# An even layer reordered: top-score selection unrolled, step sizes early, decay matrices on ScalarE in two buffers, query jobs a tile ahead

## The reference, cut to what matters

```python
def ssd_chunked(xh, dt, a, bm, cm):                  # chunks of 128 tokens, 8 heads, 2 groups
    x = (xh * dt[..., None])
    acum = jnp.cumsum(dt * a, axis=2)                # inside a chunk
    seg = acum[:, :, :, None] - acum[:, :, None]
    decay = jnp.exp(jnp.where(causal, seg, -jnp.inf))
    cb = jnp.einsum('bctgn,bcsgn->bctsg', cm, bm)
    y_diag = jnp.einsum('bctsgh,bcsghp->bctghp', cb[..., None] * decay, x)
    to_end = jnp.exp(acum[:, :, -1:] - acum)
    chunk_states = jnp.einsum('bclgn,bclghp->bcghpn', bm, x * to_end[..., None])
    ...                                              # scan: state * exp(acum[-1]) + chunk state
def dsa_attention(q, k, v, iq, ik, iw, rel_bias):
    score = sum over 4 index heads of relu(iq . ik) * iw         # 512 x 512, causal
    _, sel = lax.top_k(score, 128)                   # 128 keys for each query
    ...                                              # softmax attention over the selected keys
```

## Time and profile before

| | us |
|---|---|
| median of 3 runs | 1755.28 |
| lowest, highest | 1754.5, 1756.51 |
| the profiled execution, device time | 1753.81 |
| its span, first to last instruction | 1752.1 |
| TensorE busy | 1600.9 |
| VectorE busy | 448.1 |
| ScalarE busy | 388.9 |
| GpSimd busy | 199.5 |

### The profile page before, as it was taken

One profiled execution on the slowest core, in us unless ns is written; L12 is line 12 of the kernel. 1 busy time (PEld: TensorE's weight loads), 2 busy tenths in 40 slices (PEclk: granted clock), 3 DMA queues, 4 the chain that ended last, 5 costly groups with the idle time before them and its releaser, 6 DMA issues.

```text
span 1752.1 us, 20849 instructions
## 1 busy us (share of the span) xinstructions
PE 1600.9 (91%) x7890; PEld 757.1 (43%) x7890; DVE 448.1 (26%) x1152; ACT 388.9 (22%) x857; POOL 199.5 (11%) x286
## 2 busy tenths in 40 slices
PE   6995989979999999998399989999799999999993
PEld 3543665533333333333245447774433333333331
DVE  1475752430000000000403235552600000000002
ACT  2343252311111111111100125641211111111110
POOL 2240230000000000000101013320000000000000
PEclk9997989989999999999599999999899999999997
DMA  7120026259999999999813320024499999999995
GB/s 240 50 94 6 27 86 248 101 229 414 422 421 421 422 422 422 422 423 405 268 11 110 119 64 1 1 82 207 155 397 422 421 422 421 422 422 421 423 421 204
DMA packets 110919, 468.24 MB, mean 267 GB/s; under 512 B 34105, under 2 KB 40505, under 8 KB 61708
## 3 DMA queue, kind: packets, MB, share of 16 engines
q1 hardware_dynamic: 103564, 450.67, 64.3%
q10 hardware_dynamic: 2176, 8.39, 1.3%
q0 software_dynamic: 5120, 8.41, 1.3%
HBM read 456.91 MB, written 18.91 MB: 272 GB/s over the span
## 4 chain that ended last, share of the span: by engine, by line
PE 74%; DMA 10%; DVE 8%; issue 2%; SPq 2%; ACT 2%; POOL 1%; DVEq 0%; ACTq 0%; POOLq 0%
PE bank L1685 22%; PE bank L1698 10%; PE bank L1665 9%; PE bank L1333 8%; DMA arena<-in_moe_w_up 8%; PE bank L533 6%; PE bank L427 4%; PE bank L395 3%; PE bank L773 2%; PE bank L1675 2%; DVE arena L1113 2%; SPq L1637 2%; DVE m L1112 2%; PE bank L412 1%; PE bank L1691 1%
## 5 line engine op out<-in xcount | busy, mean ns | idle before, releaser
L1685 PE MATMUL bank<-arena 128*64 128x512 f32 x2048 | 452.7, 595 | 16.4 <-DMA arena<-in_moe_w_up 15.0
L1685 PEld LDWEIGHTS bank<-arena 128*64 128x64 f32 x2048 | 148.0, 137 | 311.7 <-issue 302.5
L1698 PE MATMUL bank<-arena 128*64 128x512 f32 x1024 | 230.6, 593 | 2.1 <-DVE arena L1787 2.1
L1783 DVE TENSOR_TENSOR arena<-arena,bank 128x256 f32<-128x256 f32 x64 | 27.0, 421 | 655.6 <-ACT arena L1773 655.6
L1704 POOL DMA_INDIRECT y_d<-arena,slot_row x64 | 62.6, 978 | 927.6 <-ACT arena L1778 914.0
L1665 PE MATMUL bank<-arena 128*64 128x512 bf16 x1152 | 153.7, 395 | 8.2 <-DVE arena L1658 8.2
L1333 PE MATMUL bank<-arena 128*128 128x512 f32 x320 | 140.7, 602 | 0.8 <-issue 0.8
L1698 PEld LDWEIGHTS bank<-arena 128*64 128x64 f32 x1024 | 71.6, 137 | 124.3 <-issue 110.8
L1773 ACT ACTIVATE arena<-bank 128x256 f32<-128x256 f32 x64 | 24.5, 383 | 420.1 <-PE bank L1685 420.1
L533 PE MATMUL bank<-arena 128*128 128x512 f32 x256 | 111.4, 593 | 0.0
L773 PE MATMUL bank<-arena 128*128 128x512 f32 (+1 forms) x288 | 106.8, 532 | 0.0
(11 more groups left out here) (279 smaller groups left out, 1450.6 us busy)
## 6 DMA issues: line engine op xcount, KB each, us to landing
arena<-in_moe_w_gate SPq DMA_DIRECT2D x64, 2048.0 KB, 21.0
arena<-in_moe_w_up SPq DMA_DIRECT2D x64, 2048.0 KB, 25.5
arena<-in_moe_w_down SPq DMA_DIRECT2D x64, 2048.0 KB, 24.2
arena<-in_even_w_in SPq DMA_DIRECT2D x4, 2048.0 KB, 8.5
arena<-y_d ACTq DMA_DIRECT2D x8, 1024.0 KB, 8.6
arena<-bias_row_d SPq DMA_DIRECT2D x2, 3584.0 KB, 11.9
arena<-in_odd_w_in SPq DMA_DIRECT2D x3, 2048.0 KB, 7.9
arena<-in_even_w_out SPq DMA_DIRECT2D x2, 2048.0 KB, 7.9
```

The costliest lines, as they stand in the source:

```text
L1685: mm = nc.tensor.matmul(bank[1][fh * CAP:(fh + 1) * CAP, :], xeT[:, j, half * CAP:(half + 1) * CAP], wgu[u][:, :, n, fh * FH:(fh + 1) * FH ...
L1698: mm = nc.tensor.matmul(bank[3][dh * CAP:(dh + 1) * CAP, :], hidT[:, j, fh * CAP:(fh + 1) * CAP], wd[u][:, n, dh * 512:(dh + 1) * 512], st ...
```

## The change

1. `take(i)` is written out: 16 pairs of `max` and `match_replace` in a straight line for each tile, no loop.
2. The three instructions of `raw_dt` stand ahead of the index scores. ScalarE's `softplus` stands after the taps of the fifth channel job. VectorE finishes `dt` and `dA` after tile 1 of the selection, and copies `acum`, `alast` and their difference after tile 2, for all tiles at once. TensorE makes the cumulated sums and the totals (with the matrix of ones) and the first tile's decay columns between the channel jobs and the z jobs. ScalarE takes the exponentials of all tiles at once, after the z jobs.
3. The x and B rows of the four tiles are turned into six different banks or halves (`x_bank`, `b_bank`), and evacuated in six copies where there were eight.
4. `seg` has two buffers. ScalarE makes it from the bank, as Relu(acum - column) and then Exp with scale -1 (8 Relus and 2 Exps for a tile); the 8 VectorE instructions, the copy of the last column and the subtraction go.
5. TensorE runs the query job of tile i+1 ahead of the state, decay and diagonal work of tile i; query head sums, scaling, turning and evacuating happen inside the loop, one or two tiles behind. `ssm_row(i-1)` moves behind seg times product of tile i, so that VectorE doesn't wait for the power at the end of a tile.
6. The four turns of Mamba rows move from before the attention's first unit to after its third to sixth group (`2 + i`), each with a wait for the last `ssm_row`. TensorE doesn't wait for `ssm_row` before the attention.
7. SyncE doesn't wait for the turned keys before it loads the second half of the output weight.

```diff
                 else:
                     self.finished(pe, u["needs"])
+                    if u["ready"]:
+                        pe.wait_ge(*u["ready"])
                     for k in range(4):
                         mm = nc.tensor.transpose(b[:, k * P:(k + 1) * P], u["src"][:, k * P:(k + 1) * P], ident[:])
...
-        seg = at(O_SS, SG, 4, P)
+        seg = [at(O_SS, SG, 4, P), at(O_SCORE + (NT - 1) * SEQ, SG, 4, P)]
         cbm = at(O_SS + 1024, SG, P)
...
         y2 = at(O_SS + 2304, DI)
         ssm_gain = at(O_SS + 2816, DI)
-        krn = at(O_SS + 3328, NT, P)
...
+
+            def queries(i):
+
+                b = q_bank(i)
+                if i in (0, 1):
+                    pe.wait_ge(S("tok_out"), (2, 4)[i])
+                else:
+                    pe.wait_ge(*((S("tok_out"), 5) if i == 2 else (S("sq"), 3)))
+                for k in range(KD):
+                    mm = nc.tensor.matmul(b[:, :], hT[:, k, i * P:(i + 1) * P], ew[0][:, k, :],
...
+            pe.wait_ge(S("dA"), 1)
+            pe.wait_ge(S("ix_relu"), len(SC))
+            for n, t_ in enumerate((tri, ones)):
+                mm = nc.tensor.matmul(bank[4][:, n * NT * SH:(n + 1) * NT * SH], t_[:], dA[:].rearrange("p i h -> p (i h)"),
+                                      start=True, stop=True)
+            mm.then_inc(S("acum_mm"), 1)
+            decays(0)
+            pe.wait_ge(S("ep_w3"), 16)
+            for i in range(NT):
+                tokens(J_Z + i, ew[1], (i,), DI)
+
+            pe.wait_ge(S("ep_ev"), J_Q)
+            pe.wait_ge(S("silu"), CT)
...
+            for i in range(NT):
...
+                    mm = nc.tensor.transpose(x_bank[i][:, j * P:(j + 1) * P], xbcS[:, j, i * P:(i + 1) * P], ident[:])
+                mm.then_inc(S("tok_turned"), 1)
+            for pair in range(2):
+                if pair:
+                    products(0)
...
+                for i in range(2):
...
+                mm.then_inc(S("tok_turned"), 1)
+            pe.wait_ge(S("ep_w4"), 16)
+            queries(0)
+            for i in range(NT):
+                if i < NT - 1:
+                    queries(i + 1)
                 if i >= 1:
                     pe.wait_ge(S("state"), i)
+                    pe.wait_ge(S("sq"), 2)
...
                 if i < NT - 1:
                     pe.wait_ge(S("xw"), i + 1)
+                    pe.wait_ge(S("tok_out"), 6)
...
                     mm.then_inc(S("st_mm"), 1)
+                    decays(i + 1)
+                    products(i + 1)
                 for g in range(SG):
...
+                if i == NT - 1:
+                    pe.wait_ge(S("kn"), 2)
...
+                    mm.then_inc(S("qk_turned"), 1)
                 if i >= 1:
...
+                    turn_queries(pe, i - 1)
+            turn_queries(pe, NT - 1)
             pe.wait_ge(S("qk_out"), NT + 1)
...
-            pe.wait_ge(S("ssm_row"), NT)
             even_att.pe(pe)
             outproj_pe(pe, even_att, "eo", mixT, e_wo, 0)
...
+            return i + 1 if i < 2 else i + 2
+
+        def q_bank(i):
+            return (bank[1], bank[4], bank[5], bank[4])[i]
+
+        def turn_queries(pe, i):
...
+                if c == CT // 2:
+                    softplus(act)
...
-                if i == 1:
-                    softplus()
...
+            act.wait_ge(S("acum"), 1)
+            nc.scalar.activation(eac[:], acum[:], ACT.Exp).then_inc(S("eac"), 1)
+            nc.scalar.activation(cdecay[:], alast[:], ACT.Exp).then_inc(S("eac"), 1)
+            nc.scalar.activation(to_end[:], to_end[:], ACT.Exp).then_inc(S("eac"), 1)
+            for i in range(NT):
+                act.wait_ge(S("tok_turned"), i + 1)
+                nc.scalar.activation(xtok[:, i, :], x_bank[i][:, :], ACT.Copy).then_inc(S("tok_out"), 1)
...
+            def decays(i):
+
+                if i >= 2:
+                    act.wait_ge(S("yd_mm"), i - 1)
                 for g in range(SG):
+                    act.wait_ge(S("abc_mm"), 2 * i + g + 1)
+                    for h in range(4):
...
+                        ins_ = nc.scalar.activation(seg[i % 2][:, g, h, :], bank[6 + g][:, h * P:(h + 1) * P], ACT.Relu,
+                                                    bias=acum[:, i, hh:hh + 1], scale=-1.0)
+                    ins_.then_inc(S("seg"), 1)
                     act.wait_ge(S("seg"), 2 * i + g + 1)
-                    nc.scalar.activation(seg[:, g], seg[:, g], ACT.Exp).then_inc(S("decay"), 1)
+                    nc.scalar.activation(seg[i % 2][:, g], seg[i % 2][:, g], ACT.Exp, scale=-1.0).then_inc(S("decay"), 1)
+
+            def queries(i):
                 act.wait_ge(S("ep_mm"), J_Q + i + 1)
-                nc.scalar.activation(qrows[:, i, :], bank[4 + i % 2][:, :], ACT.Copy).then_inc(S("ep_ev"), 1)
-                nc.scalar.activation(junk[:, i, :], bank[4 + i % 2][:, :], ACT.Square).then_inc(S("sq"), 1)
+                nc.scalar.activation(qrows[:, i, :], q_bank(i)[:, :], ACT.Copy).then_inc(S("ep_ev"), 1)
...
+            decays(0)
+            queries(0)
+            act.wait_ge(S("hgain"), 1)
+            for i in range(NT):
+                if i < NT - 1:
+                    queries(i + 1)
+                    decays(i + 1)
+                if i >= 2:
+                    turned_queries(i - 2)
                 act.wait_ge(S("y_gated"), i + 1)
                 for g in range(SG):
...
-            for i in range(NT):
+            head_norm(0, ssq[:, :, HEADS:])
+            for i in range(NT):
+                head_norm(i + 1, ssq[:, i:i + 1, 0:HEADS])
                 pool.wait_ge(S("y_sq"), 2 * i + 2)
...
+            dve.wait_ge(S("par_in"), 16 * 12)
...
+            v_.tensor_tensor(dt_e[:], dt_e[:], dt[:], ALU.max).then_inc(S("dt_abs"), 1)
...
-            def take(sc, n):
-                with dve.Fori(0, n // 16) as r:
-                    link.enter(r, 4)
-                    for _ in range(2):
-                        link(v_.max(m8[:], sc))
-                        link(v_.match_replace(sc, m8[:], sc, TAKEN))
-                    link.leave(n // 16)
...
+            def take(i):
+
...
+                for _ in range(TOPK // 8):
+                    link(v_.max(m8[:], sc))
+                    link(v_.match_replace(sc, m8[:], sc, TAKEN))
                 v_.tensor_scalar(selm[:, i, 0:L], sc, TAKEN / 2, NEG, ALU.is_gt, ALU.mult).then_inc(S("selm"), 1)
...
+            take(1)
...
                                     ALU.mult, ALU.mult).then_inc(S("dA"), 1)
+            take(2)
             dve.wait_ge(S("acum_mm"), 1)
-            v_.tensor_copy(acum[:], split(bank[3][:, 0:NT * SH], NT, SH)).then_inc(S("acum"), 1)
-            dve.wait_ge(S("acum"), 1)
+            sums = split(bank[4][:, 0:2 * NT * SH], 2, NT, SH)
+            link(v_.tensor_copy(acum[:], sums[:, 0]))
+            link(v_.tensor_copy(alast[:], sums[:, 1]))
+            v_.tensor_tensor(to_end[:], alast[:], acum[:], ALU.subtract).then_inc(S("acum"), 1)
+            take(3)
+
+            def key_sums():
...
-                for g in range(SG):
-                    dve.wait_ge(S("abc_mm"), 2 * i + g + 1)
-                    link(v_.tensor_copy(alast[:, 4 * g:4 * g + 4], split(bank[6 + g][:, :], 4, P)[:, :, P - 1]))
-                v_.tensor_tensor(to_end[:], alast[:], acum[:, i, :], ALU.subtract).then_inc(S("alast"), 1)
-                if i >= 1:
-                    dve.wait_ge(S("yd_mm"), i)
-                for g in range(SG):
-                    for h in range(4):
-                        hh = 4 * g + h
-                        ins_ = v_.tensor_scalar(seg[:, g, h, :], bank[6 + g][:, h * P:(h + 1) * P],
-                                                acum[:, i, hh:hh + 1], 0.0, ALU.subtract, ALU.min)
-                    ins_.then_inc(S("seg"), 1)
...
                 if i < NT - 1:
...
+                    v_.tensor_tensor(per_head(xw), per_head(xtok[:, i, :]), heads_bc(to_end[:, i, :], SD), ALU.mult).then_inc(S("xw"), 1)
...
                 for g in range(SG):
                     dve.wait_ge(S("decay"), 2 * i + g + 1)
-                    dve.wait_ge(S("cbm"), i + 1)
...
+                    sg_ = seg[i % 2][:, g]
+                    v_.tensor_tensor(sg_, sg_, cbm[:, g:g + 1, :].broadcast_to((P, 4, P)), ALU.mult).then_inc(S("mt"), 1)
                 if i >= 1:
-                    dve.wait_ge(S("eac"), 1)
+                    ssm_row(i - 1)
+                link(v_.tensor_tensor(per_head(y2), per_head(xtok[:, i, :]), heads_bc(d_skip[:], SD), ALU.mult))
+                if i >= 1:
...
-                    query_sums(i - 1)
+                query_sums(i)
+                if i == 1:
+                    scale_keys()
+                if i >= 1:
+                    scale_queries(i - 1)
...
-                dve.wait_ge(S("y_rstd"), i + 1)
...
+            scale_queries(NT - 1)
+            ssm_row(NT - 1)
             dve.wait_ge(S("T_in0"), 16)
+            dve.wait_ge(S("ssm_row"), NT)
             even_att.dve(dve, link)
...
```

(2 more changed lines are left out.)

228 lines of the change are left out of this document (96 added, 132 removed).

## The result

The changed kernel takes 1737.36 us (median of 4 executions, 1732.02 to 1738.76) where the kernel before took 1755.89 beside it (4 executions, 1754.5 to 1758.19): a ratio of 0.9891, with a 95% interval of 0.9876 to 0.9906. That is 18.5 us, faster by more than 0.2%. The profiled execution took 1732.02 us with a span of 1729.7, where before it was 1753.81 and 1752.1; between the two profiles lie 21.8 us. The prediction's sum was 21.7 us between profiles and its median 1733.

What follows compares the result with a forecast made beforehand. Bound: TensorE to 140.75, then VectorE's selection chain, with everything later following the attention's end. 24.8 won less 3.1 for the clock is 21.7 us: 1732.1 from the profile, 1733.6 against the median, given as 1733, range 1727 to 1740.

Steps and rivals of the forecast that it cites:

- B: Rival: TensorE's clock also falls at the pause after z, costing 3 us more, 1736; chance 0.13.
- C: Rival: Relu and Exp need separate tables, four more loads a tile, 2 to 4 us lost, 1736; chance 0.04.
- G: Rival: VectorE's or ScalarE's waits worse placed, one loop bubble of 3 to 8 us, 1737 to 1741; chance 0.18.
- The median: Whole kernel: profiled execution taken as 1.5 us under the median, so 1732.1 profiled became 1733.6; 1733 given.
- What bounds, and who is late: Before the Mamba loop: the chain runs through VectorE's selection; afterwards VectorE has 11.6 us to spare for `xw`.
- Selection: VectorE's unrolled selection: 0.35 us a trip, 24 trips, 8.4 us saved, none of it counted in the sum.
- Rival F: VectorE's straight-line selection is fetched too slowly, making the kernel slower, some 1770 at 1 us more a pair; chance 0.03.
- Step sizes: ScalarE's softplus, 3.1 us, hides in a 3.3 us gap of a channel job; 10.21 us of idle go.
- The loop: Mamba loop: TensorE works in sequence without waits from the first query job at 148.3 to 192.7.
- Decay matrices: ScalarE's Relus and Exps in the Mamba loop: 2.8 to 4.2 us a tile, hidden; VectorE's 2.15 leaves its path.
- The tail: From 192.7 VectorE bounds; the attention starts at 205.05 instead of 229.81, 24.8 us won in all.
- The attention and the clock: Attention's start: turns moved inside cost nothing; cold clock loses 2.6 us, plus 0.5 for tail turns, 3.1 together.

Runs made afterwards that it cites:

- the unrolling alone: Kernel before with only VectorE's selection written out as a straight line instead of a loop: 1738.46 us, ratio 0.9909.
- the early step sizes alone: Kernel before with only softplus, dt, dA and cumulated sums moved among the index scores, selection still a loop: 1736.89 us, ratio 0.9902.
- the queries not ahead: Changed kernel with the query job of tile i+1 behind the state, decay columns and products of tile i: 1743.61 us, ratio 0.9936.
- idle products: Changed kernel with unread TensorE products in the pauses after z, before the last turns and before the attention: 1728.46 us, ratio 0.9851.
- the decay matrices on VectorE: Changed kernel with the eight Relus of a tile back as VectorE instructions, Exp still on ScalarE: 1736.84 us, ratio 0.9886.
- both: Kernel with idle products, plus Mamba rows' turns again ahead of the attention and more unread products in the first 20 us: 1730.14 us, ratio 0.9866.
- turns first: Changed kernel with its four turns of Mamba rows again ahead of the attention's first unit, no unread products added: 1734.34 us, ratio 0.9888.
- the loop put back: Changed kernel with the selection as a loop again, 8 trips of two pairs a tile: 1738.48 us, ratio 0.9886.

## Why the prediction was right, and where it was off

The reported median, 1737.36, lies outside the forecast's own spread (1730.5 to 1735.5) and inside the range that was widened for B, C and G. None of their mechanisms is seen at work in the profiled execution: it has neither a fall of the clock after z, nor a table load between Relu and Exp, nor a bubble in the loop. So the range held, but no profile shows that the median lies where it does for the reasons for which the range was widened (*The median*, below).

*What bounds, and who is late.* Right. The wait for the end of the selection was the limit: taking it away by the unrolling alone or by the early step sizes alone gave 15.9 and 17.5 us. VectorE had 12.4 us to spare for `xw` (11.6 by the sum).

*Selection.* The term was mis-sized. I took the loop's price from the one gap that the trace shows as a wait, 0.35 us a trip, and the pair inside the loop, 1.65, for that of the straight line; this made 8.4 us. Measured without its other work and waits, the selection took VectorE 75.7 us before and 61.2 after, 14.5 less. A pair of 512 columns is 1.52 us in the straight line and on average 1.85 in the loop: not only the return, but also each instruction inside waits longer for the one before (0.79 from MAX8 to the value load, 127.35 to 128.14 before; 0.72 after, 121.78 to 122.50).

```profile
121.78 0.69 DVE L1167 MAX8 m<-arena 128x8 f32<-128x512 f32 x1
122.50 0.09 DVE L1168 MATCH_VALUE_LOAD arena<-m,arena 128x8 f32 x1
122.58 0.67 DVE L1168 MATCH_REPLACE8 arena<-m,arena 128x512 f32<-128x512 f32 x1
123.29 0.69 DVE L1167 MAX8 m<-arena 128x8 f32<-128x512 f32 x1
```

It ended at 144.95 where I had 148. Since this lay under TensorE's work, the error cost the forecast nothing; for the unrolling alone it would have. (The text ahead of the prediction calls the loop one of 8 trips a tile; in the code it is two of 4. The 24 trips in all stand.) Rival F fell: inside a tile the straight line runs without a gap. What I had not foreseen is VectorE's 2.47 us of waiting for softplus between tiles 1 and 2.

*Step sizes.* Right in the outcome. `softplus` stands after the taps of the fifth channel job, with one table load of 1.28 us where the sum had two, so it takes 1.9 us and not 3.1, and 1.86 us of idle are left before the next copy. The cover held, and it is larger than I wrote: 6.9 less 0.6 less 2.6 is 3.7, not 3.3, and the gaps without softplus are 3.61 and 3.62 (before 106.15 and 113.02).

```profile
95.90 1.28 ACT L958 ACT_TABLE_LOAD   x1
97.20 0.23 ACT L958 ACTIVATE dt_e<-dt_e 128x32 f32<-128x32 f32 x1
99.28 0.60 ACT L971 ACTIVATE arena<-bank 128x512 f32<-128x512 f32 x1 [1.86 <-PE bank L774]
```

Sums and first columns stand at 112.82 to 115.05, z ends at 142.68 (142.9 to 143.1 by the sum), TensorE goes on at 144.63 (145.0), and the first query job is at 147.95 (148.3).

*Clock at the pause after z (B).* In the first profile it did not fall: 1.00 in both windows, and the turns took 1.94 us for 16, full rate, behind a pause of 1.95 us. But this is chance too, and B was not refuted. Up to here the kernel with the queries not ahead does the same work, and in its profile the clock fell behind the same pause (0.66 in 145 to 150):

```profile
145.02 3.33 PE L875 MATMUL bank<-ident,arena 128*128 128x128 f32 x16 [1.95 <-issue]
```

The first query job then comes 1.4 us later, where B had 3. Of the six profiles with this pause and no idle products one has the fall; the early step sizes alone have it too, behind a pause of 2.00 us (0.57 in 143 to 147).

*The loop.* Right: no wait of TensorE to 192.6 (192.7 by the sum). That this hangs on the order is what the queries not ahead showed; I had costed the order as a mere sequence, and it carries 8.6 us of the way to the attention, 3.1 of them the two decay columns at half rate.

*Decay matrices (C).* C fell: ScalarE's Relus follow at 0.29 us each and the exponential comes without a table load between them. A tile takes 3.5 us of it (2.8 to 4.2 by the sum), and those of the last tile are done at 193.15, in time for VectorE, which takes them at 195.12 (195.2 by the sum). With that the trace agrees with what the Trainium skill says of relu's tables (*ScalarE: Activation LUTs*, Table sets). The rule of the same page, in Rules for kernel authors, to use VectorE and not ScalarE for relu, made the way to the attention 2.06 us longer in this kernel where it was followed (the decay matrices on VectorE); the timed runs show no difference.

```profile
149.91 1.18 ACT L1037 ACTIVATE arena<-bank,acum 128x128 f32<-128x128 f32 x4
151.12 0.63 ACT L1041 ACTIVATE arena<-arena 128x512 f32<-128x512 f32 x1
```

*The tail.* Last scaled queries at 203.06 (203.1 by the sum), the attention at 205.70 (205.05, without the cold turn's 0.5). One of the two last turns ran at half rate (1.11 us against 0.66); the earlier one at 201.31 did not.

*The attention and the clock.* Here two terms were off. I counted the turns inside the attention at nothing and the cold start at 2.6 us. Measured, the turns inside cost 1.2 us with idle products (both against idle products alone), 1.0 without them (turns first against the changed kernel's first profile, the chance of the cold start included), and the cold start 1.5 and 3.2 in two profiles of the same kernel (51.48 and 53.25 less 50.02; with the loop put back 3.4, with the queries not ahead 1.6, with decays on VectorE 1.3). In the first profile turns and cold start make 2.7, near the 2.6 of the sum only because the one came out small and the other was left out; in the repeated one they make 4.4. Where the turns' 1.2 us arise was not followed to a single wait: the trace after has small pauses of 0.30, 0.30 and 0.26 us before turns and values at 217 to 231; the two of 0.30 are missing where the turns stand first.

*The median.* The forecast for the profile was 0.1 us off, and that closeness is luck: against the sum the start gave 0.3 more and the tail with its cold turns 0.5 less, the part behind the token counts gave 0.9 of which the sum knows nothing, and the span shortened by 0.6 more than the device time. The forecast for the median was 4.4 off. I had placed the profiled execution 1.5 us under the median, as before. After the change it is 5.3 under: of nine executions of the changed kernel (1732.02 to 1738.89) three lie at 1732.0 to 1733.5 and six at 1736.5 to 1738.9. The step that failed is this carrying over from one profiled execution to the median: it took a single draw's distance for a constant, and the profiled execution happened to be the shortest of the nine. The profiles name four stretches with a chance of half speed: at the start (4.5), after z (1.4), at the attention's start (up to 2) and in the odd layer (1.6). The first is in a profile of the kernel before too; the last is in the unrolling alone, which leaves the code there as it was. Which of them make the long executions long stays open, since every profile of the unaltered changed kernel is of a short one. Nor do the runs show that it is worse off than the kernel before in this: 29 executions of that beside the runs spread from 1751.4 to 1761.3, the lowest 3.8 under their median; the nine have their lowest 4.5 under theirs.

## What to carry to other kernels

Before two edits are credited with a wait, ask whether both end the same one: here they gave 83 and 91% of the whole change's gain, each alone. A step that overlaps two engines' work in turn (the query job ahead of the state) is worth the waits that the other order would have, not the sequence's length; work out the other order as well. And read a single profile as one draw: compare distances between milestones, and take differences of a few microseconds in a total only from several timed executions.

## What the runs showed of the hardware

TensorE at half rate comes by chance in the same program: 1.87 or 3.57 us for the same four matmuls at 22 us of the kernel before, and 1.94 or 3.33 us for the same 16 turns behind the same pause of 1.95 us in two kernels that don't differ up to there. In the stretch at 22 us the column of the granted clock can't be trusted; with the loop put back it says 1.00 from 18 to 27 us, while the four matmuls take 3.57. In the profile with idle products they take 3.57 as well, and there the column says 0.50 (third and fourth line):

```profile
22.86 3.57 PE L789 MATMUL bank<-arena,relb 33*8 33x512 f32 x4 [0.83 <-issue]
...
18.00:27.00 9.00, 6.96 (x17) 3.31 (x18) 3.13 (x5) 2.07 (x4) 0.00 (x0) 1.00 0.80 175
...
22.45 3.57 PE L789 MATMUL bank<-arena,relb 33*8 33x512 f32 x4 [0.83 <-issue]
...
22.00:26.00 4.00, 3.55 (x5) 0.43 (x5) 0.34 (x1) 0.59 (x1) 0.00 (x0) 0.50 0.66 7
```

The duration of a matmul of known shape is the surer sign. And useless products in pauses of 0.8 to 3 us paid for themselves: 16 matmul instructions, 7.1 us of TensorE's time where it had nothing else, came with a median 8 us lower, of which 2.9 to 4.1 are seen in the traces.
